# A gated recurrence interleaved with its own projection in a two-block transformer kernel, with norms, short convolution and modulation loads rearranged

## The reference, cut to what matters

```python
q, f, i, g = split(h @ w_in)            # 1024 columns each
forget = lb + (1 - lb) * sigmoid(f)     # lb is 0 with one such layer
k = (1 - lb) * sigmoid(-f)
# per head (8 heads of 128): o_t = sum over s <= t of
#   (q_t * prod(forget over s+1..t)) . k_s  times the row i_s
o = rms_norm(o, out_gain) * silu(g);  y = o @ w_o
...
# short_gated_conv
z = gate_c * u
conv = sum(conv_w[j] * zp[:, j:j + S] for j in range(3))
y = (gate_b * conv) @ w_out
...
# modulation of each sublayer of the first block
mod = (silu(c) @ ada_w[layer] + ada_b[layer])   # 144 tiles of 128 outputs
```

## Time and profile before

| what | value |
|---|---|
| runs before | 3210.26 us median of 3 (3208.83 to 3215.37) |
| the profiled execution's own time | 3215.89 us |
| its span | 3214.1 us |
| PE busy in the span | 2969.8 us |
| DVE busy | 2195.5 us |
| ACT busy | 1375.9 us |
| POOL busy | 462.1 us |
| mean granted clock of TensorE | 0.96 |

### The profile page before, as it was taken

The page is one execution under the profiler, slowest core; times in us unless marked ns, Lnnn a source line. Parts: engine busy times, 40 slices in busy tenths (PEclk is TensorE's granted clock), DMA queues, the critical chain, the costliest instruction groups (busy, mean ns, idle before and its releaser), DMA issues.

```text
span 3214.1 us, 47473 instructions
## 1 busy us (share of the span) xinstructions
PE 2969.8 (92%) x18180; PEld 2606.9 (81%) x18180; DVE 2195.5 (68%) x3158; ACT 1375.9 (43%) x1473; POOL 462.1 (14%) x244
## 2 busy tenths in 40 slices
PE   3999789999895899889999999999969999999999
PEld 2887568878774788669999988888759999988887
DVE  6887678866778655656978765566566978765565
ACT  3444434444343444344444444444434444444443
POOL 0310003111000011002880000000004860000000
PEclk9999789999997999889999999999989999999999
DMA  6786247845770255214556665677434556665675
GB/s 258 281 286 222 73 172 280 295 169 194 263 268 1 104 184 170 105 66 158 183 183 218 233 229 190 241 271 264 157 118 159 183 183 235 233 215 194 243 284 204
DMA packets 146920, 640.40 MB, mean 199 GB/s; under 512 B 12472, under 2 KB 46304, under 8 KB 90352
## 3 DMA queue, kind: packets, MB, share of 16 engines
q1 hardware_dynamic: 126960, 568.02, 50.5%
q10 hardware_dynamic: 19840, 70.79, 6.1%
HBM read 604.14 MB, written 34.62 MB: 199 GB/s over the span
## 4 chain that ended last, share of the span: by engine, by line
PE 83%; DVE 8%; DMA 4%; ACT 3%; issue 2%; SPq 0%; DVEq 0%; ACTq 0%
PE pp L470 23%; PE pp L472 11%; PE pp L816 8%; PE pp L817 8%; PE pp L818 8%; PE mz L882 6%; PE mz L885 6%; PE mz L884 6%; PE mz L858 2%; DMA raw<-expert_v 2%; DMA ada_raw<-ada 2%; DVE w_lo L1372 1%; ACT w_hi L998 1%; PE mz L460 1%; DVE ada_raw L1402 1%
## 5 line engine op out<-in xcount | busy, mean ns | idle before, releaser
L1372 DVE TENSOR_TENSOR w_lo<-raw,w_hi 128x2048 fp32r<-128x2048 f32 (+1 forms) x422 | 924.1, 2190 | 479.2 <-ACT w_hi L998 478.6
L998 ACT ACTIVATE w_hi<-raw 128x2048 fp32r<-128x2048 f32 (+1 forms) x486 | 894.2, 1841 | 544.0 <-DMA raw<-expert_v 369.0
L470 PE MATMUL pp<-hs,w_hi 128*128 128x512 f32 x2400 | 872.6, 407 | 38.2 <-DVE hs L1422 37.8
L472 PE MATMUL pp<-hs,w_lo 128*128 128x256 f32 x2400 | 679.8, 283 | 0.0
L470 PEld LDWEIGHTS pp<-hs,w_hi 128*128 128x128 f32 x2400 | 456.0, 190 | 170.5 <-issue 44.7
L816 PE MATMUL pp<-hs,w_hi 128*128 128x256 f32 x2048 | 584.8, 286 | 0.0
L817 PE MATMUL pp<-hs,w_hi 128*128 128x256 f32 x2048 | 579.4, 283 | 0.0
L818 PE MATMUL pp<-hs,w_lo 128*128 128x256 f32 x2048 | 579.2, 283 | 0.0
L1977 POOL TENSOR_TENSOR w_lo<-raw,w_hi 128x2048 fp32r<-128x2048 f32 x64 | 319.0, 4997 | 1086.0 <-ACT w_hi L998 1086.0
L472 PEld LDWEIGHTS pp<-hs,w_lo 128*128 128x128 f32 x2400 | 461.2, 192 | 1.0 <-issue 1.0
L882 PE MATMUL mz<-w_hi,w_split 128*128 128x512 f32 x1024 | 400.9, 392 | 11.5 <-DVE w_split L1734 11.5
(11 more groups left out here) (297 smaller groups left out, 3076.3 us busy)
## 6 DMA issues: line engine op xcount, KB each, us to landing
raw<-expert_u SPq DMA_DIRECT2D x128, 1024.0 KB, 4.9
raw<-expert_v SPq DMA_DIRECT2D x128, 1024.0 KB, 4.9
raw<-ffn_in SPq DMA_DIRECT2D x88, 1024.0 KB, 4.9
ada_raw<-ada ACTq DMA_DIRECT2D x120, 512.0 KB, 5.6
raw<-ffn_down SPq DMA_DIRECT2D x64, 704.0 KB, 5.3
raw<-out_w SPq DMA_DIRECT2D x16, 1024.0 KB, 4.8
raw<-hgrn SPq DMA_DIRECT2D x16, 1024.0 KB, 4.9
raw<-query SPq DMA_DIRECT2D x16, 1024.0 KB, 4.8
```

Source lines behind the costliest of these rows:

```text
L470: mm(outp, w_hi[:, slot, a:a + P], rhs[:, k0 + k].rearrange("p a t -> p (a t)"), start=(k0 + k == 0), stop=False, skip_group_check=True)
L472: last = mm(outp[:, 0:T], w_lo[:, slot, a:a + P], rhs[:, k0 + k, 0, :], start=False, stop=(k0 + k == last_k), skip_group_check=True)
L998: f(w_hi[:, slot, 0:n], raw[:, slot, 0:n], ACT.Copy).then_inc(hi_ready, 1)
L1372: v.tensor_tensor(w_lo[:, slot, 0:n], raw[:, slot, 0:n], w_hi[:, slot, 0:n].bitcast(F32), ALU.subtract)\
```

## The change

It has six parts.

1. **The recurrence runs inside its projection.** The weight order becomes gate, query, output gate, value. Decays are products of the sigmoid gates themselves (`forget`); POOL multiplies them into spans of length 2, 4, ... (`spans`), so logarithm, scan, differences and exponentials go. Each level doubles the block length and updates queries (`qd`, DVE) and keys (`kd`, POOL) in place. The eight heads form four groups of two. In chunk c, group g does level c - 4 - g: groups 2 and 3 between the two tile products of the chunk (`within`), groups 0 and 1 behind it (`behind`). The level's matmuls have 64 moving columns. The last four chunks are the values, computed with tokens on partitions (48 matmuls of 256 columns a chunk), so the transposes go. The output norm runs by group inside chunks 13 to 15 and in the first part of the following `out_product` (`recurrence_closing`).
2. **Norms.** The squares become the weights and one column of ones moves (16 matmuls of 1 column, result 128x2); root and reciprocal work on 128x2; two fp32 matmuls of 128 columns spread the result into PSUM, where DVE reads it.
3. **First pair of a projection** (`first_pair`). For the first four feature tiles PE does all four tile products of both chunks, then the rest. ACT and DVE split the next pair's weights ahead of the first evacuation.
4. **Modulation.** `MOD_PLAN` takes the steps away from the recurrence and from the last pair of three `ffn_down` phases and gives 22 to `ffn_in` 2.
5. **Convolution** (`short_conv`). The weight order interleaves c and u tiles; DVE does a tile's product and taps right behind its chunk, gates and splits run in the last four chunks.
6. **`out_product`** takes an order of parts (`opening`), and loops are cut so that first or last pairs are written out.

```diff
-MOD_PER = {("ffn_in", 0): 1, ("ffn_down", 0): 1, ("attn", 0): 1, ("out", 0): 2, ("ffn_in", 1): 1, ("ffn_down", 1): 1,
-           ("ffn_down", 2): 1, ("hgrn", 0): 1}
+MOD_PLAN = {("ffn_in", 0): (1, 11), ("ffn_down", 0): (1, 7), ("attn", 0): (1, 6), ("out", 0): (2, 2), ("ffn_in", 1): (1, 11),
+            ("ffn_down", 1): (1, 7), ("ffn_in", 2): (1, 11), ("ffn_down", 2): (1, 7)}
...
-                    last = mm(mz[:, 0, 0:T], ones, sq[:, k, :], start=(k == 0), stop=(k == KD - 1), skip_group_check=True)
+                    for tb in range(TB):
+                        last = mm(mz[:, 0, tb:tb + 1], sq[:, k, tb * P:(tb + 1) * P], ones[:, 0:1], start=(k == 0 and tb == 0),
+                                  stop=(k == KD - 1), skip_group_check=True)
                 if b == KD:
                     last.then_inc(norm_sum, 1)
+                    pe.wait_ge(norm_inv, n + 1)
+                    for tb in range(TB):
+                        last = mm(mz[:, 0, T + tb * P:T + (tb + 1) * P], inv_rms[:, tb:tb + 1].to_broadcast([P, P]), ident,
+                                  start=True, stop=True, skip_group_check=True)
+                    last.then_inc(norm_wide, 1)
...
+            def first_pair(ph, n):
...
+                for k in range(KD // 2):
+                    pe.wait_ge(hs_ready, KD * n + k + 1)
+                    for j in range(2):
+                        for t in range(2):
+                            part(j, t, k)
...
+                def level(i, g):
+                    m = 1 << (i - 1)
+                    pe.wait_ge(q_up[g], i)
+                    pe.wait_ge(k_up[g], i)
+                    if i > 1:
+                        pe.wait_ge(kept[g], i)
...
+                            last = mm(mz[:, g, a:a + P // 2].rearrange("p (n r) -> p n r", r=m), kd[:, h, tok],
+                                      qd[:, h, tok].rearrange("p (n r) -> p n r", r=2 * m)[:, :, m:2 * m], start=True, stop=True,
+                                      skip_group_check=True)
...
+                def within(c):
+                    for g in (2, 3):
+                        if 1 <= c - 4 - g <= LEVELS:
+                            level(c - 4 - g, g)
+                    if 6 <= c <= 7:
+                        diagonal(c - 6)
+                    if c >= 14:
+                        spread_group(c - 14)
+                    if c >= 13:
+                        weigh_group(c - 13)
+                def behind(c):
+                    for g in (0, 1):
+                        if 1 <= c - 4 - g <= LEVELS:
+                            level(c - 4 - g, g)
+                    if 7 <= c <= 8:
+                        diagonal(c - 5)
+                    if c >= 13:
+                        sum_group(c - 13)
...
+                def grow(i, g):            # POOL; DVE has the same for qd
+                    m = 1 << (i - 1)
+                    pool.wait_ge(level_mm[g], i + 1)
+                    k_, s_ = halves_at(kd, g, m), span_of(g, m)
...
+                    g_.tensor_tensor(k_, k_, s_[:, :, :, 1:2].to_broadcast([P, 2, n, m]), ALU.mult).then_inc(k_up[g], 1)
...
-            v.tensor_tensor(ysum[:], ysum[:], pj[:, 0:8], ALU.mult).then_inc(mix_ready, KD)
-            split_mix(3, ysum[:])
+            short_conv()
```

More of the change, by code:

```diff
@@ new lines, in recurrence_closing @@
+            def recurrence_closing(part):
+                part(0, 0)
+                part(0, 1)
+                weigh_group(3)
+                part(0, 2)
+                part(0, 3)
+                spread_group(2)
+                part(1, 0)
+                part(1, 1)
+                sum_group(3)
+                part(1, 2)
+                part(1, 3)
+                spread_group(3)
+                for k in (4, 6):
+                    for j in range(2):
+                        part(j, k)
+                        part(j, k + 1)
@@ L969, in _ @@
-            out_product(1, 4)
+            recurrence(4)
+            out_product(1, 4, recurrence_closing)
             ffn(3, 5)
@@ L1029, in load_modulation @@
                     return
-                if isinstance(step, int) and step == 2 * ph.pairs:
+                if isinstance(step, int) and step >= 2 * MOD_PLAN[(ph.kind, ph.index)][1]:
                     return
@@ L1070, in ffn @@
                 load_modulation(ph, 0, 0)
-                for rp, pair, half, lap in pairs_of(act, ph):
+                for rp, pair, half, lap in itertools.chain(pairs_of(act, ph.part(0, 6)), pairs_of(act, ph.part(6, 2))):
                     for j in range(2):
@@ L1224, in swa_attention, with short_conv, high @@
                 high(HEADS - 1)
+            def short_conv():
+                ph = plan[("conv", 0)]
+                def high(i):
+                    act.wait_ge(mix_ready, KD * 2 + 2 * i + 2)
+                    f(us[:, 2 * i:2 * i + 2, 0, :], ysum[:, 2 * i:2 * i + 2], ACT.Copy).then_inc(mix_hi, 2)
+                for rp, pair, half, lap in each_pair(ph):
+                    for j in range(2):
+                        c = 2 * rp + j
+                        closing = c == 2 * ph.pairs - 1
+                        if rp == 0 or closing:
+                            split_next(ph, rp, pair, half, lap, j)
+                        take_cross(ph, ph.evac0 + c, j, 2 * pair + j + 1)
+                        if closing:
+                            high(2)
+                        elif rp:
+                            split_next(ph, rp, pair, half, lap, j)
+                        if KD < c < 2 * ph.pairs - 1:
+                            high(c - KD - 1)
+                high(3)
             def peer(l, n):
@@ L1388, in projections @@
             def projections(ph):
-                for rp, pair, half, lap in pairs_of(dve, ph):
+                for rp, pair, half, lap in itertools.chain(pairs_of(dve, ph.part(0, 1)), pairs_of(dve, ph.part(1, ph.pairs - 1))):
+                    opening = isinstance(rp, int) and rp == 0
                     for j in range(2):
+                        if opening:
+                            split_next(ph, rp, pair, half, j)
                         add_halves(pj[:, bass.ds(4 * rp + 2 * j, 2), :], ph.evac0 + 2 * rp + j, j)
-                        split_next(ph, rp, pair, half, j)
+                        if not opening:
+                            split_next(ph, rp, pair, half, j)
                         modulation(ph, rp, j)
```

617 lines of the change are left out of this document (394 added, 223 removed).

## The result

The changed kernel takes 3105.8 us (median of 4 runs, 3098.2 to 3111.0) against 3212.0 us for the kernel before. The ratio is 0.9667, with a 95% interval of 0.9644 to 0.9690: 3.3% faster. A second comparison gave 3100.4 us and 0.9652 (0.9633 to 0.9671). The forecast was 3100 us, the range 3076 to 3130. The profiled execution took 3111.0 us with a span of 3109.1, so 105.0 us of span went, where the sum of the prediction had 110.5.

A forecast was written before the change was run, and what follows sets the result against it. PE was taken to set the time nearly everywhere. Savings 63 + 8 + 7 + 8 + 24.5 = 110.5 us from 3215.9 give 3105.4; with the median of runs 5.6 lower, the forecast was 3100 us, range 3076 to 3130.

The forecast's parts named there:

- Part 1: Recurrence: 200.7 us become 137.8, made of 132.8 of PE work, 3 of waits, 2 of low clock; 63 us saved.
- The wait at `spread_group(0)`: Recurrence, chunk 14: PE waits 1.2 us for `invert(0)`, which stands on DVE behind the split of chunk 13.
- C: Rival: PE's clock falls inside the recurrence because small matmuls fill 3.6 of 9.15 us; 27 us more, 3127; chance 0.06.
- A: Rival: POOL sets the recurrence's pace, a grow taking 3 us; 26 us more, 3126; chance 0.13.
- D: Rival: slower than before, POOL grows in the recurrence taking 6 us each; 3234 us; chance 0.03.
- Part 5: Convolution: the 22.7 us wait and the low clock behind it go, 0.5 us booked against; 24.5 us saved.
- Part 2: Ten norms: 0.8 us saved in each gap, 8 us; narrow sums booked at nothing, bound 0.3 us a norm.
- rival B: The clock stays up after norms, regaining eight times 2 us; 3084 us; chance 0.13.
- Part 4: Modulation: clearing the last pair of three `ffn_down` phases saves 2.7 us each, 8 us; bounds 0 and 11.
- the excess of 2.6 to 4.3 us a phase: Extra time of modulated `ffn_down` over unmodulated, placed at the phase's end, before the last addition to x; 2.7 us taken.
- Part 3: First chunk pair behind norms: 3 us of waits saved, 2 lost to low clock; 1 us each, 7 us over seven norms.
- E: Rival: off-path gains only, norms and modulation returning nothing; 3123 us; chance 0.09.

The follow-up runs named there:

- second profile of after: The changed kernel, unaltered, run once more against the kernel before: 3100.4 us, ratio 0.9652.
- fill_gap: spread_sums plus unread filler products in every norm, one before the wait for the reciprocal, three behind the spreading: 3090.8 us, ratio 0.9613; again 3089.3 us, 0.9616.
- fill_more: fill_gap plus three more filler products ahead of the wait for the last squares of each norm: 3085.8 us, ratio 0.9602.
- spread again: spread_sums run once more, in one comparison with the last runs on one chip: 3099.7 us, ratio 0.9643.
- spread_sums: The changed kernel with the first seven one-column sums of `ffn_down` in four places instead of two: 3096.1 us, ratio 0.9626.

## Why the prediction was right, and where not

**The sum.** 110.5 us forecast from 3215.9, and 104.9 measured between the two profiled executions. By stages it is 61.7 (recurrence) + 6.9 (gaps) + 7.9 (phases between the norms, most of which begin with a first pair) + 2.1 (`ffn_down`) + 24.5 (convolution) = 103.1 of the 105.0 us of span. The other 1.9 us are the stretch from the first product behind norm 9 to the end, 3.5 us shorter (822.2 before, 818.7 after), less 1.5 us by which the first norm comes later. Luck has a share: of the 7.9 us, 3.4 lie in `ffn_in` 1, and 2.2 of these are chunks of 5.55 instead of 5.65 us (below), which the second profile of after does not have.

**Part 1, right.** Recurrence with its out product took 224.1 us before and takes 162.4: 61.7 us saved, 63 forecast. Without the out product's own 23.4 us, 139.0 us stand against 137.8. Chunks 9 and 10 are 9.13 us against 9.15, so 0.227 us for a small fp32 product holds at 64 moving columns. The wait at `spread_group(0)` is 0.3 us, not 1.2. The largest wait, 2.0 us at the third chunk of the out product, was not in the working. A POOL growth is 0.70 us (0.74 forecast), a DVE growth 0.56 (0.42), and DVE needs 6.2 us a chunk (6.3). C is excluded by the clock of 0.99, A and D by 0.70 us a growth.

**Part 5, right.** 24.5 us forecast and measured. The projection of the convolution takes 70.1 us with PE busy throughout.

**Part 2, right in the gaps, wrong in the sums.** The gaps gave 6.9 us (8 forecast; 0.5 in the gap of norm 5). The step that failed is the one that booked the narrow sums at nothing with 0.3 us a norm as bound. It looked only at their own duration. A run of twelve of them brings the clock down behind it. Over the 13 profiles of after and its variants the clock fell in 17 of 24 `ffn_down` phases with such a run and in 1 of 28 without (before's four have none either). I had used that very observation against rival B (the clock there is 0.50 from 1058.6 to 1062.0 us, behind the run) and did not carry it to the sums inside `ffn_down`.

**Part 4, mis-sized: 8 us forecast, 2.1 measured.** The three modulated phases went from 213.6 to 209.8 us, and the fourth lost 1.6. The second profile of after has 0.7 us in place of 2.1. The mis-sized term is the excess of 2.6 to 4.3 us a phase, which the prediction put at the phase's end. In the kernel before, the wait for the last squares is 3.40, 3.65 and 3.35 us in the three modulated phases and 1.54 in the fourth, so 1.8 to 2.1 us a phase lie there; `ffn_down` 0 and 2 have another wait of 1.3 and 1.4 us in their course. That end wait did go: it is 1.54 or 1.55 us in all four phases after, 5.8 us less in sum. The mechanism is right: with the sums spread and the last pair cleared the three take 204.7 us, and not cleared 215.2. But the low clock delays the last products, and the wait that the clearing takes away is covered by that delay. The two hid each other: with the other in place, each is worth 7 to 10 us in the profiles of the first comparisons (3 us for the spreading in the profiles of the last). In the time of the whole program the repair (spreading) gave 10 us in one comparison and 1 in another. So how much of it lasts is open: squares that come late in some executions, behind a reduction that waits for its data, cost PE up to 3 us a phase.

**Part 3, right.** 8 us over eight norms (7 and the recurrence's 1) against 8.4 to 8.8 over nine first chunks. The clock is low behind most norms, as said: rival B did not occur. fill_gap and fill_more show that B's mechanism exists once PE is kept busy through the norm; it was worth 10 to 14 us against spread again, and 5 in the first comparison, where B had 16.

**E** is excluded: gaps and first pairs gave 15 us.

## What to carry to other kernels

When work is put on the engine that sets the time, ask what it does to the clock behind it, not only how long it takes: here twelve products of one column in a row took no longer than the six wide ones in their place, and the cost stood behind them. Two repairs at the same point can cover each other, so each is tried with the other in place before it is called worthless. Where a dependent chain must leave TensorE idle between two dense phases, dense products that nothing reads, short enough to end before the operands arrive, can pay for themselves, as they did here: of the three runs with fillers, each against its own base, one (fill_more) is shorter beyond the intervals, and the two others are shorter within them.

## What the hardware showed that was not expected

- **Narrow products lower the clock without a wait.** Twelve fp32 products with one moving column, 2.84 us back to back, were followed by 3.4 to 6.8 us at 0.50 of the clock (1.2 GHz) in 17 of 24 phases. The Trainium skill (TensorE: Matmul & The Clock Gate, Part 1) says that a hardware block gates the clock by how busy PE has been. The fillers' effect agrees. PE counts as busy in the profile throughout such a run and still loses the clock, so a busy share of 100% in the profile did not vouch for the clock here. Whether it is the single column or the new weights of each such product that matter, no run separates.
- **Fillers keep the clock.** Seven dense fp32 products of 128x256 in a norm left the clock at 1.00 behind it where it was 0.76, and the program 13.9 us shorter than the same kernel without them (3085.8 against 3099.7). Over the 6.8 us from the first product behind the eight later norms that a first pair follows, the clock was 0.87 to 1.00 in that profile, and 0.59 to 0.77 in that of spread_sums.
- **Two paces of one chunk.** 32 dense products take 5.55 or 5.65 us, mostly the same one through a phase, and a phase changes sides from one execution to the next (`ffn_in` 1: 5.55 in one profile of after, 5.65 in the other). On a phase of 22 chunks that is 2.2 us. I found no cause.
